# The border between two blocks: first q and k on the unscaled operand, and work handed between VectorE and GpSimd

## What is computed

```
hn = rms_norm_2(x, norm_gain)
aq, ak, av, ag, rq, rk, rv, rg = split(hn @ w_in)     # 8 parts of 512
ya = chunked_rel_attention(aq, ak, av, rel_bias)      # 8 heads of 64
yr = chunkwise_retention(rq, rk, rv, cos, sin)        # 4 heads of 128
x  = x + concat(ya * silu(ag), yr * silu(rg)) @ w_out
```

## Time and profile before

| | |
|---|---|
| median of 3 runs | 1226.86 us (1225.43 to 1226.87) |
| the profiled execution's own time | 1226.96 us |
| its span in the profile | 1225.2 us |
| PE busy | 1206.4 us (98%) |
| DVE busy | 843.0 us (69%) |
| ACT busy | 553.2 us (45%) |
| POOL busy | 345.7 us (28%) |

### The profile page before, as it was taken

The page is one execution under the profiler, slowest core; times in us unless marked ns, Lnnn a source line. Parts: engine busy times, 40 slices in busy tenths (PEclk is TensorE's granted clock), DMA queues, the critical chain, the costliest instruction groups (busy, mean ns, idle before and its releaser), DMA issues.

```text
span 1225.2 us, 15010 instructions
## 1 busy us (share of the span) xinstructions
PE 1206.4 (98%) x5822; PEld 1012.5 (83%) x5822; DVE 843.0 (69%) x1534; ACT 553.2 (45%) x954; POOL 345.7 (28%) x267
## 2 busy tenths in 40 slices
PE   9999999999999999999999999999999999999997
PEld 7878888888888888888887789888888889888886
DVE  5768735466887546653669866778967766778964
ACT  6657532324444224333444456644335555553433
POOL 0135289997000000000003753342003033342000
PEclk9999999999999999999999999999999999999999
DMA  8222233222233323233222332222222332222221
GB/s 302 79 93 70 71 111 91 98 92 98 87 97 110 104 86 103 88 102 103 82 90 88 109 108 93 86 87 78 78 71 101 105 106 89 95 85 83 77 70 69
DMA packets 35912, 117.43 MB, mean 96 GB/s; under 512 B 3968, under 2 KB 4480, under 8 KB 35840
## 3 DMA queue, kind: packets, MB, share of 16 engines
q1 hardware_dynamic: 35552, 116.28, 29.2%
q10 hardware_dynamic: 288, 0.18, 0.0%
HBM read 114.35 MB, written 2.10 MB: 95 GB/s over the span
## 4 chain that ended last, share of the span: by engine, by line
PE 74%; DVE 16%; ACT 6%; issue 2%; POOL 1%; DMA 0%; SPq 0%; ACTq 0%
PE ps L280 72%; DVE RA L257 7%; DVE FA L257 4%; ACT RA L249 3%; DVE FA L269 2%; ACT FA L254 1%; ACT RA L253 1%; DVE RA L269 1%; POOL FA L257 1%; DVE FA L1337 1%; PE ps L1371 1%; PE ps L809 0%; DVE FA L1341 0%; ACT FA L253 0%; DMA FA<-w_units 0%
## 5 line engine op out<-in xcount | busy, mean ns | idle before, releaser
L280 PE MATMUL ps<-RA 128*128 128x512 f32 (+1 forms) x5470 | 1183.1, 376 | 10.4 <-DVE RA L257 5.0
L280 PEld LDWEIGHTS ps<-RA 128*128 128x128 f32 x5470 | 974.4, 189 | 196.7 <-DVE RA L257 5.7
L257 DVE TENSOR_TENSOR RA<-FA,RA 128x1024 fp32r<-128x1024 f32 (+5 forms) x317 | 342.4, 1090 | 168.5 <-ACT RA L249 166.5
L249 ACT ACTIVATE RA<-FA 128x1024 fp32r<-128x1024 f32 (+4 forms) x337 | 279.5, 857 | 341.7 <-PE ps L280 157.5
L257 POOL TENSOR_TENSOR FA<-FA 128x512 f32<-128x512 f32 (+1 forms) x89 | 120.1, 1350 | 524.3 <-ACT FA L253 423.7
L273 POOL TENSOR_SCALAR FA<-FA 128x256 f32<-128x256 f32 (+2 forms) x117 | 146.1, 1260 | 179.6 <-DVE FA L277 176.9
L269 DVE SCALAR_TENSOR_TENSOR FA<-ps,FA 128x512 f32<-128x512 f32 (+3 forms) x137 | 98.1, 720 | 90.4 <-PE ps L280 45.0
L254 ACT ACTIVATE FA<-FA 128x512 f32<-128x512 f32 (+4 forms) x109 | 60.3, 554 | 99.4 <-DVE FA L1341 78.4
L269 DVE SCALAR_TENSOR_TENSOR FA<-FA 128x4 f32<-128x4 f32 (+4 forms) x166 | 81.1, 494 | 20.5 <-ACT FA L249 7.1
L253 ACT ACTIVATE FA<-ps,FA 128x512 f32<-128x512 f32 x56 | 38.1, 684 | 108.3 <-PE ps L280 108.3
L253 ACT ACTIVATE FA<-FA 128x512 f32<-128x512 f32 (+2 forms) x79 | 45.0, 576 | 63.1 <-DVE FA L269 47.0
(11 more groups left out here) (43 smaller groups left out, 273.1 us busy)
## 6 DMA issues: line engine op xcount, KB each, us to landing
FA<-w_units SPq DMA_DIRECT2D x189, 512.0 KB, 3.4
FA<-rel SPq DMA_DIRECT2D x16, 256.0 KB, 3.4
FA<-w_units SPq DMA_DIRECT2D x8, 384.0 KB, 3.0
FA<-x SPq DMA_DIRECT2D x8, 256.0 KB, 5.5
FA<-x_rows SPq DMA_DIRECT2D x4, 512.0 KB, 9.4
FA<-dmat SPq DMA_DIRECT2D x8, 256.0 KB, 3.2
out<-FA SPq DMA_DIRECT2D x8, 256.0 KB, 2.2
FA<-w_units SPq DMA_DIRECT2D x2, 256.0 KB, 4.1
```

The costliest lines, as they stand in the source:

```text
L249: return lambda eng: eng.activation(dst, src, ACT.Copy)
L257: return lambda eng: eng.tensor_tensor(dst, a, b, op)
L280: return lambda e: e.matmul(dst, a, b, start=start, stop=stop_)
```

## The change

The operand with the features' gain alone gets a region of its own (`XBH`, `XBL`), so that scaled and unscaled operand exist side by side, and SBUF use grows by 768 columns of the tile region. On it:

- Layer 1's k0 and then q0 run on the unscaled operand right behind the four v units (in `plan()` k0 comes ahead of q0). Their results are multiplied by the token factors on the way out of PSUM (one more DVE instruction each, into a tile in SBUF, from which they are then split). The first unit on the scaled operand is q1.
- The transposes of the moments move from between v units 0 and 1 to the middle of v unit 1; the spreads of both factors move to behind v unit 2. `normalise` no longer waits for the v units. Its eight tiles are spread: 0 to 2 after v2, 3 and 4 after v3, 5 after k0, 6 and 7 after q0, in one round with the split of q0.
- The last of the plain additions, `f1a.7`, is on DVE.
- `z` and `x1` are queued one tile a slot in slots 2 to 9.
- The splits of the values are made two after k0 and two after q0.
- The low parts of nine weight units per layer (q0, v7, k5, q6, q7, k7, g5, g6, g7) are made on POOL.
- At the start of block 1 the low part of the last tile (k = 7) is made on DVE.

```diff
-R_COLS = Z + 29952
+XBH, XBL = Z + 22528, Z + 26624
+R_COLS = Z + 30720
+POOL_LOW = {f"{l}{u}" for l in range(2) for u in ("q0", "v7", "k5", "q6", "q7", "k7", "g5", "g6", "g7")}
...
-        u.append((f"{l}q0", tall(wi, item_col(0, "q"))))
-        u.append((f"{l}k0", tall(wi, item_col(0, "k"))))
+        for w in ("kq", "qk")[l]:
+            u.append((f"{l}{w}0", tall(wi, item_col(0, w))))
...
-                V(f"wl.{v}", [f"wh.{v}"], sub(R(l, n), F(RAW + 1024 * (v % 3), n), Rf(h, n)))
+                (G if keys[v] in POOL_LOW else V)(f"wl.{v}", [f"wh.{v}"], sub(R(l, n), F(RAW + 1024 * (v % 3), n), Rf(h, n)))
...
-            return normalise("x0", k, PV + PV_G1, "rn", "rn", (V, G)[k % 2])
+            return normalise("x0", k, PV + PV_G1, "rn", "rn", G if k in (1, 3, 5) else V)
...
-            A(f"fg.{m}", [f"fh.{m}", "gg", "gemm.uv21"], func(R(xh(m)), F(H + 512 * m), ACT.Copy, scale=gain))
+            A(f"fg.{m}", [f"fh.{m}", "gg", "gemm.d1.7"], func(R(XBH + 512 * m), F(H + 512 * m), ACT.Copy, scale=gain))
...
-                G(f"f1a.{m}", [f"f1q.{m}", "f2a.0"] + ([f"f1a.{m - 1}"] if m > 1 else []), add(F(ACC), F(ACC), F(t)))
+                (G if m < 7 else V)(f"f1a.{m}", [f"f1q.{m}", "f2a.0"] + ([f"f1a.{m - 1}"] if m > 1 else []), add(F(ACC), F(ACC), F(t)))
...
+                if g == 1 and l == 0:
+                    midway.append(first_moments)
...
+                    if g == 2:
+                        spread_scale()
+                        spread("r1b", RC, 5, ["f1.rc"])
+                        normal([0, 1, 2])
+                        A("r1", ["r1b"], copy(F(OB), bank(5)))
+                        free("bank5", "r1")
+                    if g == 3:
+                        normal([3, 4])
+                    continue
...
+            def scale_residual(k):
+                hk = F(H + 512 * k)
+                G(f"z.{k}", [f"f1q.{k}", f"0x.f{k}"], ts(hk, hk, F(PV + PV_GF + k, 1), ALU.mult))
+                G(f"x1.{k}", ["r1", f"z.{k}"], mul(hk, hk, F(OB)))
...
             if l == 0:
-                free("ob", "x1.7")
+                gemm_tall("0k0", 7, lambda k: XBH + 512 * k, lambda k: XBL + 512 * k)
+            else:
+                gemm_tall(f"{l}q0", 6, xh, xl, 8, normed)
...
+                if i == 0 and l == 0:
+                    t, tn = t_slot()
+                    V(f"{key}.n", after + ["0rn"] + take(tn), mul(F(t), bank(b), F(RB)))
+                    free(f"bank{b}", f"{key}.n")
+                    after, place = [f"{key}.n"] + room, (t, tn)
...
-            gemm_tall(f"{l}k0", 7, xh, xl)
-            staggered([evac_qk(0, "q", 6, f"{l}q0"), evac_qk(0, "k", 7, f"{l}k0")])
+            if l == 0:
+                rounds([normal_of(5), evac_qk(0, "k", 7, "0k0")])
+                gemm_tall("0q0", 6, lambda k: XBH + 512 * k, lambda k: XBL + 512 * k)
+                rounds([normal_of(6), normal_of(7), evac_qk(0, "q", 6, "0q0")])
+                split_values(range(2, 4))
+            else:
+                gemm_tall("1k0", 7, xh, xl)
+                staggered([evac_qk(0, "q", 6, "1q0"), evac_qk(0, "k", 7, "1k0")])
...
+                if l == 0 and 2 <= s < 10:
+                    scale_residual(s - 2)
```

More of the change, by code:

```diff
@@ L426, in gemm_first, with token_major @@
                                                              i == 0 and n == 0, False))
-        def token_major(key, ks, places, colw, first, last, xafter=None):
+        def token_major(key, ks, places, colw, first, last, xafter=None, high=XH, low=XL):
             u = unit(key)
@@ L1203, in two_blocks_kernel, with normal_of, rounds, normal @@
             rcol = R12 if l == 0 else RC
+            raw_h, raw_l = (XBH, XBL) if l == 0 else (XH, XL)
+            def normal_of(k):
+                return normalise(f"{pre}x", k, gcol, f"{pre}rn", "gemm.uv21" if l == 0 else f"gemm.{l}v{k // 2}")
+            def rounds(chains):
+                for _ in range(2):
+                    for c in chains:
+                        next(c, 0)
+            def normal(ks):
+                staggered(normal_of(k) for k in ks)
+            def first_moments():
+                turn_squares("f1", ACC, 4, ["f1a.7"])
+                free("f1", "f1.sT")
+                turn_squares("f2", SG, 5, ["f2a.7"])
+                sum_squares("f2", 5, SS2)
+                sum_squares("f1", 4, SS)
+                V("f1.ms", ["f1.ss"], ts(F(MS, 4), F(SS, 4), 1.0 / 1024, ALU.mult, 1e-5, ALU.add))
+                V("f2.a", ["f2.ss"], ts(F(MS2, 4), F(SS2, 4), 1.0 / 1024, ALU.mult))
+                V("f2.b", ["f1.ms"], ts(F(RC2, 4), F(MS, 4), eps, ALU.mult))
+                V("f2.ms", ["f2.a", "f2.b"], add(F(MS2, 4), F(MS2, 4), F(RC2, 4)))
+                bit_rstd("0rcol", None, MS2, R12, TMP, ["f2.ms"], None, None, V)
+                bit_rstd("f1.rc", None, MS, RC, TMP2, ["f1.ms"], None, None)
@@ L1204, in two_blocks_kernel, with spread_scale @@
+            def spread_scale():
+                spread(f"{pre}rb", rcol, 4, [f"{pre}rcol"])
+                A(f"{pre}rn", [f"{pre}rb"], copy(F(RB), bank(4)))
+                free("bank4", f"{pre}rn")
             for g in range(4):
+                if g == 1 and l == 0:
+                    midway.append(first_moments)
                 token_major(f"{l}v{g}", [2 * g, 2 * g + 1], [(t, 0) for t in range(4)], 512,
[L1206 to L1217, removed]
-                    V("f2.ms", ["f2.a", "f2.b"], add(F(MS2, 4), F(MS2, 4), F(RC2, 4)))
-                    bit_rstd("0rcol", None, MS2, R12, TMP, ["f2.ms"], None, None, V)
-                    bit_rstd("f1.rc", None, MS, RC, TMP2, ["f1.ms"], None, None)
@@ L1247, in two_blocks_kernel @@
[L1247 to L1252 removed]
+                    spread_scale()
+                normal(NORMALISED[g])
+            def scale_residual(k):
+                hk = F(H + 512 * k)
+                G(f"z.{k}", [f"f1q.{k}", f"0x.f{k}"], ts(hk, hk, F(PV + PV_GF + k, 1), ALU.mult))
+                G(f"x1.{k}", ["r1", f"z.{k}"], mul(hk, hk, F(OB)))
+                if k == 7:
+                    free("ob", "x1.7")
@@ L1254, in item_cols @@
+            split_values(range(2) if l == 0 else range(4))
             def item_cols(i):
```

46 lines of the change are left out of this document (19 added, 27 removed).

## The result

The changed kernel takes **1216.97 us** (median of five runs, 1216.83 to 1217.13) against 1226.87 before (also of five): a ratio of 0.9922, with a 95% interval of 0.9912 to 0.9933. The gain is 9.9 us where 5.75 were forecast. The time lies inside the range, near its lower end, at the number that rival (a) had named. It did not get there in rival (a)'s way. The profiled execution took 1217.13 us, with a span of 1215.0.

What follows compares the result with a forecast made beforehand. PE's work was taken as the bound (busy 1206.4 of 1225.2 us), leaving some 19 us of waits; start 0.65, border 3.9 and late slots 1.2 sum to 5.75, giving 1221.1 us, range 1216.6 to about 1225.0.

Steps and rivals of the forecast that it cites:

- rival (a): POOL's 1024-column subtractions run beside DVE with no hold to speak of: 9.65 us gained, 1217.2 us; chance 0.22.
- late slots: Late in each layer, low parts on POOL shrink three PE waits: -0.3 to +1.4 us per layer, 0.6 taken twice, 1.2 gained.
- The start: Block 1's start: x's last low part on DVE cuts PE's wait from 1.62 to about 1.0 us, 0.65 gained.
- The moments and the clock: Border between blocks: the 1.85 us wait ahead of the moments' transposes goes, and with it the fall of the clock.
- k0 and q0 first: Border: q0's inner waits go, new waits of 1.4 us in q1 and 0.9 before the scores; border gains 3.9 us.
- neither wait would be left: Border: if POOL's subtraction did not hold DVE, the waits in q1 and before the scores vanish and the gain is 6.2 us.
- The residual scaling: Sixteen POOL operations spread over slots 2 to 9 cost 0, as DVE has time left there.
- the worse branch of the forecast: Third late break: g6's low part on POOL falls into the rsqrt chain's small two-input steps; 1.19 becomes about 1.4 us.
- The better branch: Third late break: g6's low part misses the rsqrt chain's small steps, DVE is early and the 1.19 us wait is gone.
- (b): Border: the new wait in q1 throttles the clock, 1.6 us less gained, 1222.7 us; chance 0.09.
- (c): Late slots: seven low parts each hold DVE 2.5 us to save 1.21, making the kernel slower, 1231.3 us; chance 0.06.
- (d): Border: the moments still stop PE, f1a.7 late beyond 0.5 us of cover; about 3 us less gained, 1224; chance 0.08.

Runs made afterwards that it cites:

- f1a_pool: Changed kernel with the last plain addition f1a.7 back on POOL, the moments staying in the middle of v unit 1: 1217.08 us, 0.9928.
- border_only: Changed kernel with all weight low parts back on DVE, none on POOL: 1221.58 us, 0.9962 of the kernel before.
- q0_dve: Changed kernel with q0's low part back on DVE in both layers, the other eight on POOL: 1217.6 us, 0.9931 of the kernel before.
- residual_border: Changed kernel with the sixteen residual scaling operations on POOL moved from slots 2 to 9 back to the border: 1223.31 us, 0.9975 of the kernel before.
- q7_on: Changed kernel with the low parts of v7, k5 and q6 back on DVE, the other six on POOL: 1219.01 us, 0.9940 of the kernel before.
- low_only: Kernel before with only the nine low parts per layer moved to POOL: 1224.59 us, 0.9988.
- q1_g6: Changed kernel with layer 1's q1 low part also on POOL and g6's low part on DVE: 1216.58 us, 0.9923 of the kernel before.
- halves: Changed kernel with each low part on POOL issued as two subtractions of 512 columns: 1218.14 us, 0.9935 of the kernel before.
- moments_v0: Changed kernel with the transposes of the moments straight behind v unit 0, f1a.7 still on DVE: 1218.46 us, 0.9935 of the kernel before.

## Why the prediction was right, and where it was off

**The number: in the range, partly by luck.** The lower end of the range was taken from rival (a), whose mechanism is refuted. By the forecast's own mechanism, with its late slots at their upper end, the gain was at most 0.65 + 3.9 + 2 x 1.4 = 7.35 us and the time 1219.5; the measured 1216.97 lies below that.

**The start: right.** 1.02 us of wait were foretold as "about 1.0", and they come from DVE. Of these 0.6, 0.4 arrive at the v units; the other 0.2 were lost in the first 15 us of the program, which no edit touches.

**The moments and the clock: right, for one of two reasons.** PE reaches the transposes at 670.58 (670.8 foretold), and the clock stays at 1.00 from 670 to 675. f1a_pool shows that only the later place mattered; the sum on DVE was costed as part of the same gain and has none of its own here.

**k0 and q0 first: right in kind, 1.1 us short in size.** The two waits stand where they were put, 1.4 and 0.9 foretold, 0.53 and 0.76 measured beyond pace, from start to start less the 0.23 us of a matmul (0.37 and 0.60 as idle time in the rows). The terms that were too long: POOL's subtraction began 1.2 us earlier than assumed (685.9 for 687.1), because ACT's high part was ready sooner and the whole stage began 0.4 earlier, so that the hold ended at 688.7 and not 689.6; and ACT's copies of k0 take 0.65 each, not the 0.74 taken from the earlier trace rows. The hold itself was sized right, 2.4 for an estimate of 2.5. What it cost was wrong: the walk took 1.21 us for DVE's own step, while border_only and q0_dve, without the hold, have both waits in the same size or larger, because DVE then spends 2.2 us on the step and its waits for ACT. The other claim, that with the low part on POOL and no hold "neither wait would be left", is tested by no run. That DVE's steps and its 1.87 us wait for ACT make the two waits in every variant here is read from the timelines; no run took one of them away alone.

**The residual scaling: the cost was right, the gain had no term.** It was costed at 0 in slots 2 to 9, and that holds. But the walk through the border took every DVE step at its undisturbed length, so the 3.9 us contained the emptied POOL without saying so. residual_border prices it: 5.1 us at the border (46.6 for 41.5), as much as the border's whole gain, and 0.7 behind it. Of everything in the change, this is the edit on which the rest of the border depends.

**The late slots: the term that failed.** 0.6 per layer were taken from a span of -0.3 to 1.4; 2.4 were measured. Two steps were wrong. First, the break at 816.68 was priced at its one row of 0.16. PE's timeline of the kernel before goes on behind that row with the next wait of the same late chain:

```profile
817.66 1.57 PE L280 MATMUL ps<-RA 128*128 128x384 f32 x6 [0.24 <-DVE FA L1341]
```

Held against the same matmuls of the changed kernel, PE lost 0.3 us up to the first row, 0.5 from there to the second and 0.3 right behind it, 1.1 in all, and the lead grew by that when they went. Second, each break was given the relief of the low part nearest to it. DVE's lateness is carried on from unit to unit: v7's, k5's and q6's low parts, off DVE long before the second break, moved the steps there 1.8 us earlier against PE, so that break vanished where I had it grow from 0.76 to 1.0. q7_on shows it: with those three back on DVE, the break is 1.07. The third break went the way of the worse branch of the forecast, with 0.15 + 0.73 where 1.4 were said; the 0.5 us below that I can't assign to one step. The better branch, "the wait is gone", is what q7_on shows. By the ledger of the spans the gain is 10.2 for 5.75, and of these 4.45 us more, 3.6 are this term, 1.1 the border and -0.25 the start.

**The rivals.** (a) named the time and is refuted in its mechanism: the hold was seen at 686.49 and 856.28. (b) did not occur in the changed kernel, whose new waits were at most 0.73 us; low_only and residual_border show what it would have looked like. (c) did not decide: the late slots gain as a whole. Its mechanism is there, in two places: a hold that meets a chain with no slack (g6, and q1 in q1_g6) costs about 1 us more than DVE's own step each time. (d) did not occur.

**The rules of the Trainium skill.** The Trainium skill's GPSIMD Engine Reference, 3.1 Elementwise, gave by half of its 2048-column time an estimate of 2.25 us for POOL's subtraction; the rows say 2.39 to 2.42, for the most part, between that and my 2.5. The Trainium skill's SBUF — State Buffer, SBUF: two separate sides, has a shared pair of ports held for the whole instruction by whichever starts first, a GpSimd operation that reads SBUF or a DVE operation with two SBUF inputs. For two-input GpSimd operations the rows agree (2.77 at 686.49, 2.44 at 856.28, and in halves one small step held by each instruction). For the one-input half of the residual scaling they don't: in residual_border DVE's two-input step at 692.22 ends at 693.39, while POOL's one-input operation runs from 692.16 to 693.73. A step held for the whole of it could not have ended before that; it took 1.17 us for 0.74.

## What to carry to other kernels

When work is taken off an engine that is late, follow that engine's lateness from the first unit that changes to the last, and let each relief carry on to all later waits; a break's price is PE's whole loss against its pace around it, not the one row with the bracket. Price a hold against what the held engine would have done instead, its own step and its waits included: the same 2.4 us cost nothing at q0, 1.1 at q1 and 1.0 a layer at g6, and at g6 nothing where it began 0.25 us behind the chain, so move a weight's low part to POOL one unit at a time and keep it off places where a short dependent chain runs. And when a walk through the steps uses undisturbed lengths, write down which other edit makes them undisturbed, for that edit carries the gain.

## What the runs showed of the hardware

- An operation of four columns on DVE can be held as long as one of 512: two such steps took 2.44 us beside a POOL subtraction of 2.39 and 0.36 without it. With the subtraction in two halves of 1.30 and 1.29 us, each half held one step, for 1.31 and 1.21 us: DVE got through between them, and its next step was caught.
- Where a one-input POOL operation ran beside DVE's two-input steps in residual_border, DVE's step at 692.22 took 1.17 us for 0.74 and ended before POOL's, which took 1.57, as one did in the changed kernel at 735.62 beside a DVE step that reads PSUM. In other places of residual_border POOL's operation was lengthened as well, to 2.00 to 2.53.
- In the changed kernel, too, the memset of 128x2048 on POOL (1.81 us from 665.15) left two two-input DVE steps beside it at their lengths, 0.74 us at 665.34 and 1.21 at 666.01.
- PE's granted clock was 1.00 behind waits of 1.02 us (changed kernel), 1.24 (moments_v0), 1.32 (before) and 1.44 (q1_g6), 0.66 in the stretch around one of 1.85, 0.50 behind one of 5.06 (residual_border), and 0.50 behind three waits of 0.84, 0.74 and 1.33 that followed each other within 5 us (low_only). The last series, with none of its waits as long as 1.85, was not expected.
